# Two rankings between the halves of the output projection, three beside dense gates, and every second quad of gate rows on POOL

## What is computed

```python
xs = xs + g1 * mixer_merge(att, four, subln_g, lam_init, w_out)   # [att | four] @ w_out
h2 = rmsnorm(xs, norm2_g) * (1 + sc2) + sh2
xs = xs + g2 * peer(h2, w_query, sub_keys, expert_u, expert_v)
# peer, for each token:
q = (hf @ w_query).reshape(T, 8, 2, 128)
s = einsum('thpk,hpnk->thpn', q, sub_keys)          # 8 heads, 2 x 128 keys
s1, i1 = top_k(s[:, :, 0], 16); s2, i2 = top_k(s[:, :, 1], 16)
top_s, pos = top_k(s1[..., None] + s2[..., None, :], 16)        # 16 experts of 128 x 128
g = softmax(top_s)
out = sum_k g_k * gelu(expert_u[ix_k] . h) * expert_v[ix_k]
```

## Time and profile before

| | us |
|---|---|
| median of 3 runs (1866.28 to 1871.09) | 1868.1 |
| the profiled execution | 1869.13 |
| its span, first to last instruction | 1867.3 |
| PE, DVE, ACT, POOL busy | 1732.7, 1519.6, 683.2, 797.7 |
| output projection, on PE | 340.8 to 411.7 |
| first ranking done, dense gates begin | 484 |
| last dense quad multiplied | 724 |
| last ranking done | 773 |
| PE's expert loop begins | 783.7 |

### The profile page before, as it was taken

One profiled execution on the slowest core, in us unless ns is written; L12 is line 12 of the kernel. 1 busy time (PEld: TensorE's weight loads), 2 busy tenths in 40 slices (PEclk: granted clock), 3 DMA queues, 4 the chain that ended last, 5 costly groups with the idle time before them and its releaser, 6 DMA issues.

```text
span 1867.3 us, 29896 instructions
## 1 busy us (share of the span) xinstructions
PE 1732.7 (93%) x9942; PEld 1483.9 (79%) x9942; DVE 1519.6 (81%) x3123; ACT 683.2 (37%) x1135; POOL 797.7 (43%) x646
## 2 busy tenths in 40 slices
PE   5999988889899998499999999999999999999994
PEld 2667656438788888499999999999999999999994
DVE  0732047245989999999999999999999999999997
ACT  1222146101477674233333333333333333333332
POOL 1111000000000000477877778877666666666661
PEclk8999999899999999699999999999999999999997
DMA  9455100700044555799999999999999999999993
GB/s 358 156 198 221 48 1 1 276 39 12 1 91 91 128 115 134 303 394 405 405 400 387 407 407 407 405 402 399 407 406 397 406 404 399 392 402 407 406 405 135
DMA packets 253543, 520.91 MB, mean 279 GB/s; under 512 B 113955, under 2 KB 130979, under 8 KB 252197
## 3 DMA queue, kind: packets, MB, share of 16 engines
q1 hardware_dynamic: 178016, 249.00, 37.4%
q0 software_dynamic: 73728, 268.47, 36.3%
q10 hardware_dynamic: 1734, 2.60, 0.4%
HBM read 488.55 MB, written 31.46 MB: 278 GB/s over the span
## 4 chain that ended last, share of the span: by engine, by line
PE 53%; DVE 24%; issue 13%; DMA 5%; ACT 3%; DVEq 1%; SPq 0%; POOL 0%; POOLq 0%; PEldq 0%; ACTq 0%
DVE arena L1214 11%; PE ps L1594 9%; PE ps L1593 9%; PE ps L1592 9%; PE ps L1512 5%; PE ps L1493 4%; PE ps L1563 4%; DMA arena_w<-in_w_mod 2%; PE ps L1343 2%; DVE V_lo L1164 2%; PE ps L1347 2%; PE ps L1344 2%; DMA U_in<-in_expert_uT 2%; PE ps L1391 1%; DMA arena_w<-in_w_in 1%
## 5 line engine op out<-in xcount | busy, mean ns | idle before, releaser
L1592 PE MATMUL ps<-hT_hi,U_hi 128*128 128x384 f32 x1024 | 344.3, 336 | 13.6 <-DVE U_lo L1159 13.6
L1594 PE MATMUL ps<-hT_hi,U_lo 128*128 128x384 f32 x1024 | 344.5, 336 | 0.0
L1593 PE MATMUL ps<-hT_lo,U_hi 128*128 128x384 f32 x1024 | 343.7, 336 | 0.0
L1592 PE MATMUL ps<-V_hi,C_hi 128*128 128x512 f32 x768 | 300.5, 391 | 18.1 <-DVE C_lo L1189 18.1
L1593 PE MATMUL ps<-V_lo,C_hi 128*128 128x512 f32 x768 | 302.7, 394 | 0.0
L1594 PE MATMUL ps<-V_hi,C_lo 128*128 128x512 f32 x768 | 302.6, 394 | 0.0
L748 ACT CAST V_hi<-V_in 128x1024 fp32r<-128x1024 f32 x128 | 135.0, 1055 | 217.3 <-PE ps L1594 217.3
L1592 PEld LDWEIGHTS ps<-hT_hi,U_hi 128*128 128x128 f32 x1024 | 193.0, 188 | 18.7 <-issue 13.8
L785 ACT ACTIVATE act_t<-ps 128x384 f32<-128x384 f32 x128 | 63.0, 492 | 393.9 <-PE ps L1594 393.9
L479 POOL DMA_INDIRECT arena<-in_expert_u,idxn x128 | 170.4, 1332 | 85.8 <-issue 32.1
L479 POOL DMA_INDIRECT arena<-in_expert_v,idxn x128 | 159.3, 1244 | 93.4 <-DVE arena L1214 42.8
(11 more groups left out here) (239 smaller groups left out, 3218.8 us busy)
## 6 DMA issues: line engine op xcount, KB each, us to landing
U_in<-in_expert_uT SPq DMA_DIRECT2D x128, 512.0 KB, 9.2
V_in<-in_expert_v SPq DMA_DIRECT2D x128, 512.0 KB, 6.4
arena_w<-in_w_mod SPq DMA_DIRECT2D x12, 2048.0 KB, 12.4
gates_scratch<-arena_w SPq DMA_DIRECT2D x6, 4096.0 KB, 20.8
gate_in<-gates_scratch SPq DMA_DIRECT2D x128, 192.0 KB, 7.4
arena_w<-in_w_in SPq DMA_DIRECT2D x4, 2048.0 KB, 8.9
arena_w<-in_w_query SPq DMA_DIRECT2D x1, 7168.0 KB, 21.1
arena_w<-in_w_out SPq DMA_DIRECT2D x2, 2048.0 KB, 10.4
```

The lines of the kernel that those rows point to most:

```text
L1592: nc.tensor.matmul(out, hi, rhi, start=start, stop=False)
L1593: nc.tensor.matmul(out, hi, rlo, start=False, stop=False)
L1594: return nc.tensor.matmul(out, lo, rhi, start=False, stop=stop)
```

## The change

- The order of blocks is 0, 1, 2, 3, 4. PE's list is now halves of the projection with queries and scores of blocks 0 and 1 between them; DVE's list has the rankings of blocks 0 and 1 between `merged` (gating a half) and `make_h2`. The residual is loaded straight into `H2[b]`, and `make_h2` waits until its spill has landed.
- The rankings of blocks 2, 3 and 4 stand beside the dense gates of blocks 1, 2 and 3. In the last, PE has no query of a next block to make; DVE puts all its gate rows into the first three groups, and the split of the activations, the fourth group and `select` behind them.
- POOL makes `gate_rows` of the odd quads, DVE of the even ones.
- The last half of the table is written in three pieces (experts' rows 0 to 39, 40 to 71, 72 to 127). The first loads of `expert_v` and of the table wait for the first piece. POOL's first six gathers wait for none of it.
- The reloads of the residual (five), of the final gain and of the sparse block's `H2` are moved from ahead of the expert loop into it, and the clearing of the accumulators into its middle.

The diff, cut to its core:

```diff
+PIECES = (0, 40, 72, NKEY)
...
-ORDER = (1, 2, 3, 4, 0)
-FIN = (4, 0, 1, 2, 3)
+ORDER = (0, 1, 2, 3, 4)
+FIN = (0, 4, 1, 2, 3)
...
+def dense_at(n):
+    return n - 1 if 2 <= n <= NDEN + 1 else 0
...
-            sp.wait_ge(s_wT, len(UNITS))
+            sp.wait_ge(s_chunk_used, DFT_C + 1)
             for b in range(NBLK):
-                sp.dma_start(X[:, b], xall[b * P:(b + 1) * P, :]).then_inc(s_xr[b], 16)
+                sp.dma_start(H2[b], xall[b * P:(b + 1) * P, :]).then_inc(s_xr[b], 16)
...
+                if b == NDEN:
+                    sp.wait_ge(s_fill2, B2.total)
+                    for j in range(2):
+                        load_u(j, j)
                 for half in range(2):
-                    sp.wait_ge(s_gev, QUADS * (b - 1) + QUADS // 2 * (half + 1))
+                    sp.wait_ge(s_gev, QUADS * (b - 1) + HALFQ * (half + 1))
                     t0 = half * (P // 2)
+                    if b == NDEN and half:
+                        for e in range(3):
+                            part = slice(PIECES[e], PIECES[e + 1])
+                            sp.dma_start(gates_d[part, :, TD - P // 2:TD].rearrange("i p t -> p i t"),
+                                         gbuf[:, part, P // 2:P]).then_inc(s_glast[e], 16)
+                        break
...
-            sp.wait_ge(s_fill2, B2.total)
-            for j in range(2):
-                load_u(j, j)
-            for half in range(2):
-                sp.wait_ge(s_gout[half], 16 * NDEN)
+            for n in range(2, 4):
+                sp.wait_ge(s_ulo, n - 1)
+                load_u(n, n % 2)
+            sp.wait_ge(s_gout[0], 16 * NDEN)
+            sp.wait_ge(s_gout[1], 16 * (NDEN - 1))
+            sp.wait_ge(s_glast[0], 16)
...
-            for b in range(NBLK):
-                sp.dma_start(XF[:, b], x1_d[b * P:(b + 1) * P, :]).then_inc(s_xf, 16)
-            sp.dma_start(fing, final_g.unsqueeze(0).broadcast_to([P, D])).then_inc(s_fing, 16)
-            sp.wait_ge(s_acc0, 1)
-            sp.wait_ge(s_h2out, 16)
-            sp.dma_start(H2s, h2_d).then_inc(s_h2in, 16)
...
+            turns = PAIRS // 8
+            with sp.Fori(2, turns) as i:
+                streams(i)
+            sp.dma_start(H2s, h2_d).then_inc(s_h2in, 16)
+            for b in range(NBLK):
+                with sp.Fori((b + 1) * turns, (b + 2) * turns) as i:
+                    streams(i)
+                sp.dma_start(XF[:, b], x1_d[b * P:(b + 1) * P, :]).then_inc(s_xf, 16)
+            sp.dma_start(fing, final_g.unsqueeze(0).broadcast_to([P, D])).then_inc(s_fing, 16)
...
+                        if first and g == 0 and row == 6:
+                            pool.wait_ge(s_gout[0], 16 * NDEN)
+                            pool.wait_ge(s_glast[2], 16)
+                            pool.sem_inc(s_staged, 1)
...
+            def gate_rows(b, p):
+                q = (b - 1) * QUADS + p
+                if p == 1:
+                    pool.wait_ge(s_selT, b)
+                if q >= RR1:
+                    pool.wait_ge(s_gq, q - RR1 + 1)
+                for t in range(QUAD):
+                    at = p * QUAD + t
+                    ins = pool.tensor_scalar(rhs1[q % RR1][:, t, :], iota[:, :], selT[:, b % 2, 0, at:at + 1],
+                                             selT[:, b % 2, 1, at:at + 1], ALU.is_equal, ALU.mult)
+                ins.then_inc(s_rhs1p, 1)
+            for b in range(1, NDEN + 1):
+                for p in range(1, QUADS, 2):
+                    gate_rows(b, p)
...
+            squares2(0)
+            turned(0)
+            squares2(1)
+            query_out(0, 0)
+            query_out(0, 1)
+            turned(1)
+            squares2(2)
+            query_out(0, 2)
+            query_out(0, 3)
+            squares2(3)
+            query_out(1, 0)
+            softmax_exp(0)
+            query_out(1, 1)
+            query_out(1, 2)
+            squares2(4)
+            turned(2)
+            query_out(1, 3)
+            turned(3)
+            turned(4)
+            query_out(2, 0)
+            query_out(2, 1)
+            softmax_exp(1)
...
+            split_u(0, 0, 1)
+            split_u(1, 1, 1)
+            softmax_exp(NBLK - 1)
+            act.wait_ge(s_glast[1], 16)
...
+            def merged(b, half):
+                c, i = min(b, 1), 2 * b + half
+                if half == 0:
+                    dve.wait_ge(s_xr[b], 16)
+                cols = slice(half * NC, (half + 1) * NC)
+                dve.wait_ge(s_merge, i + 1)
+                dve.tensor_tensor(gated[:, cols], ps[:, 4 + i % 4, :], M[:, c, G1, cols], ALU.mult).then_inc(s_gated, 1)
+                dve.wait_ge(s_gated, i + 1)
+                dve.tensor_tensor(H2[b][:, cols], H2[b][:, cols], gated[:, cols], ALU.add).then_inc(s_x1, 1)
...
+                dve.wait_ge(s_spill[b], 16)
...
-                    quads[0] += 1
+                    quads[0] += 2
...
+            merged(0, 0)
+            merged(0, 1)
+            make_h2(0)
             dve.wait_ge(s_out, 32)
-            dve.wait_ge(s_spill, 16 * NBLK)
             dve.tensor_copy(identb, ident[:, :])
             dve.tensor_scalar(downb, iota[:, :], -1.0, None, ALU.mult)
             link(dve.memset(onesb, 0.0))
             dve.memset(onesb[0:1, :], 1.0)
-            for n, b in enumerate(ORDER):
-                bd = n if 1 <= n <= NDEN else 0
-                ranking(n, b, bd, (1, 2, 1), (0, 1, 1), (2, 2, 2, 3))
+            merged(1, 0)
+            merged(1, 1)
+            make_h2(1)
+            ranked(0, 0)
+            merged(2, 0)
+            ranked(0, 1)
+            merged(2, 1)
+            ranked(0, 2)
+            make_h2(2)
+            merged(3, 0)
+            ranked(0, 3)
+            merged(3, 1)
+            dve.wait_ge(s_step, steps[0])
+            select(0)
+            make_h2(3)
+            gate_weights(0)
+            ranked(1, 0)
+            merged(4, 0)
+            ranked(1, 1)
+            merged(4, 1)
+            ranked(1, 2)
+            make_h2(4)
+            ranked(1, 3)
+            dve.wait_ge(s_step, steps[0])
+            select(1)
+            gate_weights(1)
...
+            for n in range(2, NBLK):
+                bd = dense_at(n)
+                if bd != NDEN:
+                    ranking(n, n, bd, (1, 1, 0), (0, 1, 0), (1, 1, 1, 2))
+                else:
+                    for g in range(3):
+                        key_tops(n, g, bd, (1, 2, 1) if g else (0, 1, 1))
+                        dve.wait_ge(s_step, steps[0])
+                        pair_tops(g, bd, ((1, 1, 1), (0, 1, 0), (1, 1, 0))[g])
+                    dve.wait_ge(s_hThi, 1)
+                    dve.tensor_tensor(hT_lo.rearrange("p k (b t) -> p k b t", b=NDEN),
+                                      h2T[:, 1:1 + NDEN].rearrange("p b k t -> p k b t"),
+                                      hT_hi.rearrange("p k (b t) -> p k b t", b=NDEN).bitcast(f32),
+                                      ALU.subtract).then_inc(s_hTlo, 1)
+                    split_u(0, 0)
+                    ranked(n, 3)
+                    split_u(1, 1)
+                    dve.wait_ge(s_step, steps[0])
+                    select(n, 0)
...
-            dve.memset(cutout(XO, 2 * D), 0.0).then_inc(s_acc0, 1)
-            dve.wait_ge(s_acc0, 1)
             experts(0, False, dot_row(0))
             with dve.Fori(1, PAIRS // 4) as i:
                 experts(i, False, dot_row(0))
+            dve.wait_ge(s_h2in, 16)
             with dve.Fori(PAIRS // 4, PAIRS // 2) as i:
                 experts(i, False, dot_row(1))
+            dve.memset(cutout(XO, 2 * D), 0.0).then_inc(s_acc0, 1)
+            dve.wait_ge(s_acc0, 1)
             coefs(0)
             with dve.Fori(PAIRS // 2, 3 * PAIRS // 4) as i:
...
+                pe.wait_ge(s_rhs1p if q % 2 else s_rhs1, q // 2 + 1)
...
+            merge(0, 0)
+            merge(0, 1)
+            merge(1, 0)
+            turn(0)
+            merge(1, 1)
             pe.wait_ge(s_wq, 16)
             pe.wait_ge(s_wq7, 16)
             pe.wait_ge(s_keys, 16)
-            pe.wait_ge(s_act2, B2.emptied(B2.pos[("h2T", NBLK - 1, 1)])[1])
-            whole_query(ORDER[0], 0)
-            whole_query(ORDER[0], 1)
-            for n, b in enumerate(ORDER):
-                bd = n if 1 <= n <= NDEN else 0
-                if bd:
-                    selT_fill(bd)
-                ahead = [(b, 2), (b, 3)]
+            turned(0)
+            part(0, 0)
+            score(0, 0)
+            merge(2, 0)
+            part(0, 1)
+            merge(2, 1)
+            score(0, 1)
+            turn(1)
+            part(0, 2)
+            merge(3, 0)
+            score(0, 2)
+            part(0, 3)
+            merge(3, 1)
+            score(0, 3)
+            turned(1)
+            part(1, 0)
+            merge(4, 0)
+            score(1, 0)
+            part(1, 1)
+            merge(4, 1)
+            score(1, 1)
+            part(1, 2)
+            score(1, 2)
+            turn(2)
```

(10 more changed lines are left out.)

196 lines of the change are left out of this document (98 added, 98 removed).

## The result

The changed kernel takes 1886.3 us (median of four, 1884.4 to 1887.1), the kernel before 1869.4 beside it: ratio 1.0088, interval 1.0076 to 1.0100. The forecast was slower, by 6 us, in a range of 1862 to 1887. The direction and the range held; the loss is 17 us and not 6. Of the missing 10.6, 6.4 lie in one of its terms, the reloads in the loop, and 3.2 behind the last dense quad, where the table's write and with it the first load of `expert_v` came late.

What follows compares the result with a forecast made beforehand. PE was taken to bound the dense stages, the expert loop to move with its start. Terms of +37.2, -10.2 and -22.7 ahead of the loop and +2 in it gave +6.3, so 1874 us, range 1862 to 1887.

Steps and rivals of the forecast that it cites:

- What bounds what: Whole kernel: the expert loop's end moves with its start; PE bounds the dense stages at 4.43 us per two quads.
- Term 1: Rankings of blocks 0 and 1 among the halves: dense gates at 522.4 instead of 484.05, +38.3, with an 8.5 us stall.
- Terms 2 and 3: Dense stages: PE's work unchanged, start 1.1 us shorter; third stage bound by ACT near its end, finishing at 751.0.
- POOL's price: Dense gate rows on POOL: 0.55 us per instruction, between 0.24 and 0.70, hidden behind PE.
- Rival A: Dense stages: POOL is the bound, from 0.83 us per instruction in the third's end, 1.11 elsewhere; 1915 us, chance 0.12.
- 45 us a stage: Dense stages: DVE could lose up to 64 x 0.7 = 45 us each if every instruction collided with POOL's.
- POOL issues six gathers from 747: Tail: POOL issues six gathers, 3 MB, from 747 without waiting for the table; taken to cost its write 5 us.
- Term 4: Tail after 751.0: V(0) lands at 781 behind table write and gathers; loop starts at 788 (782 to 790), +4.3.
- Term 5: Work moved into the expert loop: clearing 1.9 us, reloads 1.3 us of DMA each; +2 taken, between 0 and 5.
- D: Rival: PE stalls more than walked, waiting for DVE's bank or `merged`; +10 to +15, 1886 us, chance 0.12.
- B: Rival: table write and gathers overlap, reloads hide; V(0) at 776, 1866.5 us, no change, chance 0.29.
- C: Rival: faster, the spill lands without the queue and write and gathers overlap; loop starts near 774, 1858 us, chance 0.13.

Runs made afterwards that it cites:

- e4: The kernel before with POOL making the gate rows of the odd quads and nothing else of the change: 1866.2 us, ratio 0.9976 to 0.9994.
- e3: The changed kernel with all gate rows on DVE again and none on POOL: 1880.0 us, ratio to the kernel before 1.0051 to 1.0079.
- e2: The changed kernel with the spill of block 0 issued by ACT on its own queue: 1883.5 us, ratio to the kernel before 1.0066 to 1.0094.
- e5: The changed kernel with the load of the query weights cut at three eighths around the spill of block 0: 1881.2 us.
- e6: The changed kernel with all gate rows of the last dense block on DVE, POOL's only in the first two: 1879.8 us.
- e9: The changed kernel with the first loads of expert_v and the table ahead of the third and fourth loads of U in SP's list: 1881.2 us.

## Why the prediction was right, and where it was not

- **What bounds what**: right. The loop moved with its start, apart from the reloads, and PE set the dense stages. e4 and e3 put POOL's help there at 1.3 and 1.0 us for three stages.
- **Term 1**: right to 0.1 us, with the stall (8.37 us measured, 8.5 said) and its cause, in the traces of e2 and e5. That it is carried whole was confirmed there too. What the prediction did not ask was whether the query weights had to be under way at that moment; they had not, and that was the cheapest mending.
- **Terms 2 and 3**: right, last quad at 750.7 (751.0). Quads came at 1.64 in the last stage, ACT's pace, and POOL, at 3.2 to 3.3 for every second quad, ran just level with it. DVE's busy time fell by 14.1 us in 80, not 17.7, which cost nothing.
- **POOL's price**: wrong. 0.55 was taken between 0.24 and 0.70; it is 0.80 alone and 0.90 on average. Rival A still did not come: in the first two stages 0.93 lies below its threshold of 1.11, and in the third POOL's rows took 0.81, just under the 0.83, up to the last quad, whose 5.87 us made PE wait 1.2. That it stayed under was close, and luck in part, since 0.81 lies outside the bounds that the prediction had worked out. Of the 45 us a stage that DVE could have lost by collisions it lost none that the rows show. But "POOL issues six gathers from 747" had POOL free in time, and never asked what stood ahead of them in POOL's list, nor that the new block order had made their numbers known long before.
- **Term 4**: right in its structure, short in its sizes. The write took 27.3 us to land beside the gathers (751.4 to 778.7), and 21.2 and 22.0 without, in e3 and e6, so the gathers cost 5.3 to 6.1 where 5 were said; the write was counted at 25.9 with them, 1.4 short. "Two loads of U, 1.3 us each" was right for what they add (e9: 2.9 for both), though SP needed 8.4 to issue them, which no row of before showed. V(0) came 4.7 behind the write and not 3.9 for three loads. From V(0) to the loop it was 7.6, not 7. So V(0) landed at 783.4, not 781, the loop began at 791.0, not 788, 1 us beyond the bounds. (The 775.7 without sharing is 776.0 by its own terms, 751.2, 20.9 and three loads of 1.3.)
- **Term 5**: the mis-sized term. +2, with 5 as its upper end; it is +8.4. What fell short is "1.3 us of DMA each": a reload in SP's queue, which has 39% of the rate, made the load of U behind it land 2 to 4 us later (3.3 by the estimate above), and the last two places cost 3.6 and 3.8 us of the loop. The clearing, which had been given 1.9 of the 5, costs nothing.
- The sum of what was missed is 6.4 in the loop, 3.2 between the last quad and the loop, 1.2 at the loop's ends, less a gain of 1.1 ahead of them; 0.9 is only where the first mark stood.
- The direction came of the gates' +38.3 against -34.0 behind them, sums that were right to 0.1 and to 2.2 us. The range was in part luck: 1886.3 lies 0.7 from its end, and that end stood for stalls of PE (D) that did not come.
- **Rivals**: B would have needed V(0) at 776 and free reloads; neither was so. C would have needed PE's wait ahead of the first transposes under 3 us; it was 8.37. D's stalls did not come: PE's waits were those that had been walked.

## What to carry to other kernels

Price a small load in a busy loop by its queue's share of the rate rather than by the machine's, and look at who stands behind it in that queue: on another queue it cost 0.8 us of the loop in place of 8.4, behind the loop's last load nothing. When an engine gets new work, look at what stood behind that place in its own list, here six gathers that were pushed from a harmless write into the one that everybody waits for. And count from a mark that the change cannot touch before two single executions are compared.
